# Probabilities times values in a sparse-attention trunk: one float32 product, or three float16 products of high and low halves

## The reference

```python
# A
logits = einsum('bqhd,bqkd->bhqk', qb, kg) * scale + bias
p = masked_softmax(logits, (dist >= 0)[:, None])
return einsum('bhqk,bqkhd->bqhd', p, vg)
# C, selected blocks and window
o_sel = einsum('bhqk,bqkd->bqhd', masked_softmax(lg, ...), vg)
o_win = einsum('bhqs,bsd->bqhd', masked_softmax(lw, ...), vw)
```

## Time and profile before

| | us |
|---|---|
| median of three runs | 667.53 |
| the profiled execution, own time | 668.36 |
| its span | 666.6 |
| TensorE matmul busy | 619.8 (93%) |
| VectorE busy | 379.9 (57%) |
| ScalarE busy | 324.5 (49%) |
| GpSimd busy | 222.4 (33%) |
| transposes of unit 0, start | 444.19 |
| last product of unit 47, start | 568.77 |

### The profile page before, as it was taken

One profiled execution on the slowest core, in us unless ns is written; L12 is line 12 of the kernel. 1 busy time (PEld: TensorE's weight loads), 2 busy tenths in 40 slices (PEclk: granted clock), 3 DMA queues, 4 the chain that ended last, 5 costly groups with the idle time before them and its releaser, 6 DMA issues.

```text
span 666.6 us, 9725 instructions
## 1 busy us (share of the span) xinstructions
PE 619.8 (93%) x3659; PEld 390.4 (59%) x3659; DVE 379.9 (57%) x828; ACT 324.5 (49%) x565; POOL 222.4 (33%) x161
## 2 busy tenths in 40 slices
PE   3999989998999999799999999989999999799998
PEld 2445667554346855577777667755666677433443
DVE  6424483525489997887887866532324453567411
ACT  4655454224455686550811524446576677353610
POOL 0153633512015283342432530343541221152520
PEclk9999999899589799999999999979999999999999
DMA  9245544522002431220211120121122110252411
GB/s 319 61 134 176 156 116 146 157 85 72 0 17 64 128 96 40 87 64 1 64 33 32 31 64 1 32 64 33 33 63 64 65 33 31 64 198 87 142 59 53
DMA packets 31191, 52.78 MB, mean 79 GB/s; under 512 B 2759, under 2 KB 13345, under 8 KB 31145
## 3 DMA queue, kind: packets, MB, share of 16 engines
q1 hardware_dynamic: 30985, 52.03, 25.3%
q10 hardware_dynamic: 160, 0.14, 0.1%
HBM read 50.04 MB, written 2.12 MB: 78 GB/s over the span
## 4 chain that ended last, share of the span: by engine, by line
PE 67%; DVE 18%; ACT 5%; issue 4%; POOL 3%; SPq 2%; DMA 1%; DVEq 0%; ACTq 0%; POOLq 0%
PE bank L1510 10%; PE bank L1512 10%; PE bank L1511 10%; PE bank L1701 8%; PE bank L1769 5%; PE bank L1773 4%; PE bank L1771 4%; DVE work L1247 3%; PE bank L1685 3%; PE bank L1877 3%; PE bank L1546 2%; POOL w_lo L498 2%; DVE early L1155 2%; PE bank L1896 2%; PE bank L1589 2%
## 5 line engine op out<-in xcount | busy, mean ns | idle before, releaser
L498 POOL TENSOR_TENSOR w_lo<-stage,w_hi 128x1024 f16<-128x1024 f32 (+4 forms) x76 | 149.8, 1973 | 242.0 <-ACT w_hi L711 242.0
L1701 PEld LDWEIGHTS bank<-work 128*128 128x128 f32 x616 | 75.1, 192 | 19.2 <-DVEq L1222 14.0
L1701 PE MATMUL bank<-work 128*128 128x128 f32 x616 | 79.7, 279 | 7.1 <-DVEq L1222 6.8
L711 ACT ACTIVATE w_hi<-stage 128x1024 f16<-128x1024 f32 (+4 forms) x76 | 74.5, 981 | 18.8 <-PE bank L1512 10.0
L1769 PE MATMUL bank<-hT_hi,w_hi 128*128 128x512 f16 x192 | 73.9, 385 | 1.7 <-PE bank L1773 0.9
L703 ACT ACTIVATE stage<-stage,small 128x512 f32<-128x512 f32 (+4 forms) x120 | 73.5, 662 | 2.2 <-DMA stage<-in_w_in 2.2
L1771 PE MATMUL bank<-hT_lo,w_hi 128*128 128x512 f16 x192 | 73.6, 384 | 0.4
L1773 PE MATMUL bank<-hT_hi,w_lo 128*128 128x512 f16 x192 | 73.6, 383 | 0.3
L1510 PE MATMUL bank<-w_hi,hT_hi 128*128 128x260 f16 (+4 forms) x192 | 62.1, 323 | 3.1 <-DVE hT_lo L955 1.4
L1512 PE MATMUL bank<-w_hi,hT_lo 128*128 128x260 f16 (+4 forms) x192 | 61.9, 322 | 0.0
L1511 PE MATMUL bank<-w_lo,hT_hi 128*128 128x260 f16 (+4 forms) x192 | 61.8, 322 | 0.0
(11 more groups left out here) (299 smaller groups left out, 1162.6 us busy)
## 6 DMA issues: line engine op xcount, KB each, us to landing
stage<-in_w_in SPq DMA_DIRECT2D x40, 512.0 KB, 3.6
stage<-in_c_phi_w SPq DMA_DIRECT2D x8, 512.0 KB, 3.9
stage<-in_w_branch SPq DMA_DIRECT2D x8, 512.0 KB, 3.7
stage<-in_w_out SPq DMA_DIRECT2D x8, 512.0 KB, 3.7
stage<-in_w_in SPq DMA_DIRECT2D x8, 260.0 KB, 2.8
strips<-rel_rows SPq DMA_DIRECT2D x8, 256.0 KB, 4.2
late<-in_x SPq DMA_DIRECT2D x1, 2048.0 KB, 9.2
out_x<-late SPq DMA_DIRECT2D x8, 256.0 KB, 2.0
```

The lines of the kernel that those rows point to most:

```text
L498: gp.tensor_tensor(piece_view(w_lo[:, k % PAIRS, :], c), piece_view(stage[:, piece_at[c, j] % STAGES, :], c), piece_view(w_hi[:, k % PAIRS ...
L711: nc.scalar.activation(piece_view(w_hi[:, k % PAIRS, :], c), full, ACT.Copy).then_inc(hi_ready, 1)
L1701: ins = mm(ps[:, h * P:(h + 1) * P], lhs(h), rhs(h), start=True, stop=True)
```

## The change

`probsT` becomes two float16 halves in the same bytes (2 x 512 float16 in place of 512 float32 per partition), `v_a` likewise, and a new tile `v_c` holds both halves of mixer C's values. `unit_out` then uses `product`, three float16 matmuls per block. ScalarE now writes the high half of the transposed probabilities only; VectorE's new `probs_lo(u)` subtracts it from the PSUM bank, writes the low half and frees the bank. It stands in VectorE's queue ahead of `logits(u + 2)`. `values_lo` and four ScalarE copies ahead of `exps(0)` make the halves of `v_c`; the drain of `v_a` gets a second pass.

```diff
-        v_a = sb("v_a", [P, NT, 256])
+        v_a = sb("v_a", [P, NT, 2, 256], f16)
-        probsT = [late[:, 1024 + 512 * n:1536 + 512 * n] for n in range(2)]
+        probsT = [late[:, 1024 + 512 * n:1536 + 512 * n].bitcast(f16).rearrange("p (a n) -> p a n", a=2) for n in range(2)]
+        v_c = sb("v_c", [P, NT, 2, 2, 64], f16)
...
+            values = raw_c1[:, :, 0:256].rearrange("p t (s g d) -> p t s g d", s=2, g=2)[:, :, :, 0, :]
+            for t in range(NT):
+                ins = nc.scalar.activation(v_c[:, t, :, 0, :], values[:, t, :, :], ACT.Copy)
+            ins.then_inc(vc_hi_ready, 1)
+
             exps(0)
             for u, (m, q, h) in enumerate(units):
                 if u + 1 < len(units):
...
-                drain(("pT", m, q, h), probsT[u % 2][:, 0:L], L)
+                act.wait_ge(s_filled, S.filled(("pT", m, q, h)))
+                nc.scalar.activation(probsT[u % 2][:, 0, 0:L], S.bank(("pT", m, q, h))[:, 0:L], ACT.Copy).then_inc(pT_hi_ready, 1)
...
-                ve.tensor_copy(v_a[:, t, :], ps[:, 256:512]).then_inc(v_drained, 1)
+                hold(ve.tensor_copy(v_a[:, t, 0, :], ps[:, 256:512]))
+                ve.tensor_tensor(v_a[:, t, 1, :], ps[:, 256:512], v_a[:, t, 0, :], ALU.subtract).then_inc(v_drained, 1)
...
+            def probs_lo(u):
+                m, q, h = units[u]
+                L = P * (q + 1)
+                ve.wait_ge(pT_hi_ready, u + 1)
+                ve.tensor_tensor(probsT[u % 2][:, 1, 0:L], S.bank(("pT", m, q, h))[:, 0:L], probsT[u % 2][:, 0, 0:L],
+                                 ALU.subtract).then_inc(s_drained, 1)
+
+            def values_lo():
+                ve.wait_ge(vc_hi_ready, 1)
...
+                    ins = ve.tensor_tensor(v_c[:, t, :, 1, :], values[:, t, :, :], v_c[:, t, :, 0, :], ALU.subtract)
+                ins.then_inc(vc_ready, 1)
...
             for u in range(len(units)):
+                probs_lo(u)
                 if u + 2 < len(units):
                     logits(u + 2)
+                if u == 8:
+                    values_lo()
...
-                    v = {"A": v_a[:, k, 64 * h:64 * h + 64], "sel": raw_c1[:, k, 0:64], "win": raw_c1[:, k, 128:192]}[m]
-                    ins = mm(ps[:, 64 * h:64 * h + 64], probsT[u % 2][:, k * P:(k + 1) * P], v, start=k == 0, stop=k == q)
+                    v = [{"A": v_a[:, k, a, 64 * h:64 * h + 64], "sel": v_c[:, k, 0, a, :], "win": v_c[:, k, 1, a, :]}[m] for a in range(2)]
+                    p = [probsT[u % 2][:, a, k * P:(k + 1) * P] for a in range(2)]
+                    ins = product(ps[:, 64 * h:64 * h + 64], p, v, k == 0, k == q)
```

More of the change, by code:

```diff
@@ L317, in trunk @@
         logits_ready, probs_ready, pv_done = sem("logits_ready"), sem("probs_ready"), sem("probsT_used")
+        pT_hi_ready, vc_hi_ready, vc_ready = sem("probsT_hi_ready"), sem("nsa_values_hi_ready"), sem("nsa_values_ready")
         bias_ready = sem("selected_bias_ready")
@@ L1873, in unit_out @@
                 ps = O.bank(("o", m, q)) if h else o_bank(("o", m, q))
+                if u == 16:
+                    pe.wait_ge(vc_ready, 1)
                 pe.wait_ge(s_drained, S.filled(("pT", m, q, h)))
                 for k in range(q + 1):
-                    v = {"A": v_a[:, k, 64 * h:64 * h + 64], "sel": raw_c1[:, k, 0:64], "win": raw_c1[:, k, 128:192]}[m]
-                    ins = mm(ps[:, 64 * h:64 * h + 64], probsT[u % 2][:, k * P:(k + 1) * P], v, start=k == 0, stop=k == q)
+                    v = [{"A": v_a[:, k, a, 64 * h:64 * h + 64], "sel": v_c[:, k, 0, a, :], "win": v_c[:, k, 1, a, :]}[m] for a in range(2)]
+                    p = [probsT[u % 2][:, a, k * P:(k + 1) * P] for a in range(2)]
+                    ins = product(ps[:, 64 * h:64 * h + 64], p, v, k == 0, k == q)
                 ins.then_inc(pv_done, 1)
```

## The result

| | before | after |
|---|---|---|
| median of the first runs, us | 667.53 (3 runs) | 674.83 (4 runs) |
| ratio, 95% interval | | 1.015, 1.008 to 1.0221 |
| the profiled execution, own time | 668.36 | 673.0 |
| its span | 666.6 | 671.2 |
| TensorE matmul busy | 619.8 | 612.5 |

What follows compares the result with a forecast made beforehand. TensorE bounds mixer C's units; GpSimd's split pass and join lead mixer A's chain. Mixer A +5.1, units 16-31 -2.3, exponentials 32-47 +7.0, the rest -0.7: +9.1 on 668.36, less 0.8 to the median, 676.8 us; 8-in-10 range 667.5 to 686.

Steps and rivals of the forecast that it cites:

- The ring of four instructions: Attention units: exponential, copy, low half, logits wait in a circle; 3.06 us at four blocks against 2.79; chance 0.68.
- rival that TensorE stays the bound: Mixer C: TensorE still bounds the units, so the change is faster, 658.5 us (663 if A's rings count); chance 0.11.
- The extras: Exponentials 32 to 47: weight splits at units 35 and 39 +1.0 each, `finish` 0.5 and twice 0.3, split at 45 0.2.
- The product: Values product on TensorE: three float16 passes cost 0.087 us a block against 0.21, saving 0.123 (0.03 to 0.135).
- The dear product: Rival: a float16 block costs 0.18 us or more, so narrow units gain next to nothing; 680 us, chance 0.07.
- Narrow units: Mixer C's units 16 to 31, one and two blocks wide: stay with TensorE and gain, net -2.3 us.
- mixer A: Its attention units: rings add 1.5 us from exponential 6 to 8 and 2.6 from 10 to 13; in all +5.1.
- Copies and `values_lo`: Four ScalarE copies before the first exponential +0.8 us (0.7 to 1.1); `values_lo` between exponentials 10 and 13 +0.5.
- The second pass over `v_a`: VectorE, stages after the attention: 0.42 us, falling in a 0.87 us wait for the next bank, so cost 0.
- Behind exponential 47: Rest of that unit, unit 47's own and the last product: TensorE has less left, -0.7 us.
- The rival of the clock: Idle TensorE in the attention units lowers the granted clock, +10 us over the sum, 686 us; chance 0.09.
- The sum: Whole kernel: 5.1 - 2.3 + 7.0 - 0.7 = +9.1 us, forecast 676.8.

Runs made afterwards that it cites:

- e1: The kernel after with VectorE's order turned: `logits(u+2)` ahead of `probs_lo(u)`; 669.88 us.
- e6: The kernel after with ScalarE's order turned: the high half of unit u copied ahead of `exps(u+1)`; 666.74 us.
- e5b: The kernel after with the probabilities' low half written and multiplied for only the first 128 columns of each unit; 666.35 us.
- e4: The kernel after with one pass of the values product in place of three, low halves still written and waited for; 671.37 us.
- e3: The kernel after with `logits(u+2)` ahead of `probs_lo(u)` and mixer C's values halved early; 665.74 us.
- e2: The kernel after with mixer C's values halved earlier, in idle stretches of ScalarE and VectorE; 671.45 us.
- e9: The kernel after, unchanged, run again in twelve executions; 672.83 us.
- e8: The kernel before with one wait added: VectorE starts `logits(u+2)` only after ScalarE's copy of unit u; 669.83 us.
- e11: The kernel after with both queues' orders turned, values halved early and mixer C's `finish` without two SBUF inputs; 667.24 us.

## Why the prediction was right, and where its sizes were off

- *The ring of four instructions.* Shown: by its rows, by opening it on either side (e1, e6), by shortening one member (e5b) and by taking TensorE's load away (e4). The high halves took ScalarE what the copy took, 0.57, as assumed; the row named for it has 0.67. The *rival that TensorE stays the bound* holds for four-block units only once an order is turned (e1, e3, e6).
- *Its length was the mis-sized term.* I had 3.06, 2.60, 2.11 and 1.64; measured 2.84, 2.36, 1.89 and 1.41. Two hand-overs were too dear. VectorE starts `logits` 0.61 after `probs_lo` (0.69 long), where I had put 0.69 + 0.05; and it starts `probs_lo` 0.60 after ScalarE's copy, where I had 0.57 + 0.11 from the earlier trace rows. Over fifteen units from exponential 32 that is 3.5 of the 7.0 forecast.
- *The extras* (splits, gate drains, `finish`) from 32 to 47: 42.47 less eight rings of 2.36 and seven of 2.84 leaves 3.7; I had 3.3.
- *The product.* Passes 0.03 apart, twelve in 0.35 us for four blocks against 0.84, so 0.12 a block as taken. The dear product, an estimate of 0.24 a block from the 81 ns that the Trainium skill, "TensorE: Matmul & The Clock Gate" (section "Back-to-back issue gap"), gives for a pair of load and matmul at 128 columns, did not come: with 0.03 at 64 columns here and 0.06 at 128 the trace disagrees with that figure.
- *Narrow units* gained 2.0 of the 2.3 forecast; *mixer A* lost 1.0 and 2.6 where I had 1.5 and 3.1, the difference again being the ring's length.
- *Copies and `values_lo`*: +0.91 for 0.8, and 0.66 for 0.5, both confirmed by e2. Of the four passes of `values_lo` beside GpSimd's joins the second took 1.38 and the others 0.28; no `probs_lo` exceeded 0.70. The second pass over `v_a` cost nothing: VectorE's idle time of 0.87 became 0.41, and the drains start as far apart as before (1.62).
- *Behind exponential 47* I expected a gain of 0.7 and got a loss of 0.7. What failed is the assumption that TensorE's saving is all that changes there: the granted clock fell in the branch products.

```profile
572.00:576.00 4.00, 3.10 (x21) 1.51 (x22) 3.45 (x10) 0.63 (x2) 0.70 (x1) 0.80 0.59 185
576.00:580.00 4.00, 3.59 (x15) 1.48 (x12) 1.83 (x4) 0.37 (x1) 0.72 (x1) 0.77 0.01 4
```

Where the clock stayed at 1.00 there, the same stretch took 102.4 (e2) and 102.1 (e5b) in place of 104.0, so the gain of 0.7 was there to be had.

- *The rival of the clock* came in two places. One is the stretch just named. The other is mixer A, before and after:

```profile
472.00:476.00 4.00, 4.00 (x28) 2.85 (x26) 1.64 (x7) 2.28 (x7) 1.07 (x1) 1.00 0.01 2
472.00:476.00 4.00, 3.78 (x24) 2.12 (x24) 2.14 (x8) 1.69 (x4) 1.27 (x1) 0.57 0.00 0
```

TensorE had been busy 1.78 of the 4 us in front of the second row and 2.65 in front of the first. The fall cost nothing that shows: exponential 11 to 13 takes 5.11 in after and 5.11 in e2, whose clock stayed at 1.00. None of the profiles of after has a fall in mixer C's units, and the 10 us of this rival did not come.

- *The sum*, +9.1: the ring's length is worth -4.6 (15 units from 32, five in mixer A) and the tail +1.4, which makes 5.9; extras +0.4, narrow units +0.3, copies and `values_lo` +0.3 bring it to 6.9. Executions at like clock show 6.5 to 7.0. The profiled pair has 4.6, because its after reached the attention 1.9 earlier and was 0.5 shorter than forecast up to exponential 10. The same instructions stand there, and in e9 exponential 0 moved by 10 us with the clock, so I put this down to the clock, without an experiment of its own. The forecast of 676.8 has a slip: 667.53 and 9.1 are 676.6. It came within 2 us of the measured 674.83 with the ring too long by 4.6 and the tail wrong by 1.4 the other way, so a part of its nearness is luck; that the change is slower, by the ring and in the wide units, is not.

## What to carry to other kernels

When an edit puts a new instruction between two queues, follow the waits round: if an instruction of unit u now stands ahead of one of u+1 on two engines, the two units of lead are gone and the unit is the sum of the chain. Compare that sum with the bound engine's unit before pricing any saving (here 2.84 ate a saving that would have given 2.30, while the 2.24 of e8 cost 0.3 us in all the units), and try the other order of each queue alone. Of the 4.8 us lost in the units, turning VectorE's gave back 3.8, while turning ScalarE's gave back 6.0, more than was lost. Turning both was worse than turning VectorE's alone.

## What the runs showed of the hardware

- *Two neighbours on VectorE overlap.* A pass of 0.69 with one PSUM input is followed by the next after 0.61 where that one waits for nothing, and one of 0.29 after 0.21. A sum of durations overstates a chain by 0.08 for each such pair. `probs_lo`, released by a ScalarE copy, started 0.03 after its end, where the earlier trace rows has 0.11.
- *The lock costs whoever comes second.* The addition of two SBUF inputs took 2.02 to 2.40 us where a GpSimd pass of 2.13 had started first, and that pass kept its 2.13. Where the addition had started first it took its 0.42 or 0.43, and the GpSimd pass took 2.13 to 2.35, longer the more of the addition was left. Both happen in after:

```profile
507.31 0.43 DVE L1423 TENSOR_TENSOR work<-work 128x256 f32<-128x256 f32 x1
507.46 2.26 POOL L500 TENSOR_TENSOR w_lo<-stage,w_hi 128x1024 f16<-128x1024 f32 x1 [6.00 <-ACT w_hi L713]
...
548.49 2.13 POOL L500 TENSOR_TENSOR w_lo<-stage,w_hi 128x1024 f16<-128x1024 f32 x1 [7.82 <-ACT w_hi L713]
548.87 2.03 DVE L1423 TENSOR_TENSOR work<-work 128x256 f32<-128x256 f32 x1
```

Which of the two it is depends on tenths of a microsecond and less: with starts 0.01 apart it went one way in e1 (addition 2.40) and the other in e3 (0.43, the GpSimd pass 2.42). Of the eight additions the fifth is long in before, after, e1 to e5b, e8 and e9; the first is long in e1 and e3 as well, the fourth in e1 alone; e6 has no long one. Four fused passes with one input in PSUM and one in SBUF took 0.86 where such a pass started in their midst and 0.86 without one. The Trainium skill, "SBUF — State Buffer" (section "Who interferes with whom"), tells of the exclusion; these rows agree.
- *The clock in the index scores has two courses with the same program.* In after's first profile it was 0.60 and then 0.50, the lower of the two levels (1.2 GHz of 2.4):

```profile
164.00:168.00 4.00, 3.71 (x9) 1.58 (x8) 2.08 (x5) 1.74 (x5) 0.29 (x1) 0.60 0.02 4
168.00:172.00 4.00, 3.90 (x9) 1.99 (x8) 2.47 (x4) 1.69 (x4) 0.00 (x0) 0.50 0.00 0
```

In e9's it stayed full, with TensorE less busy, so the greater busy share above is the slower clock and not more work, for the program is the same:

```profile
164.00:168.00 4.00, 3.16 (x12) 1.67 (x12) 2.69 (x6) 2.31 (x6) 0.29 (x1) 1.00 0.02 4
168.00:172.00 4.00, 3.48 (x12) 1.27 (x9) 3.18 (x6) 2.01 (x5) 0.00 (x0) 1.00 0.00 0
```

Exponential 0 comes 9.8 us earlier then. What decides between the two isn't shown: up to 164 us the two profiles have TensorE equally busy at the full clock (3.23 and then 3.02 or 3.01 of 4 us from 156 on). The fall behind the attention is as fickle: before had TensorE busy 2.82 and 2.33 of 4 us from 572 on and the clock at 1.00, e8 1.69 of 4 and a fall, e5b 1.94 and e11 1.27 of 4 and none.
